# An expert layer with 128 token slots per expert instead of 96

## The reference

```
def moe_swiglu(h, router_w, router_b, w1, w3, w2):      # h: 256 tokens x 1024
    logits = h @ router_w + router_b
    top_val, top_idx = lax.top_k(logits, 2)             # 2 of 8 experts for each token
    top_p = softmax(top_val)
    combine = sum(one_hot(top_idx, 8) * top_p[..., None], axis=-2)
    for e in range(8):                                  # w1, w3: 1024 x 3584, w2: 3584 x 1024
        out = out + combine[..., e:e+1] * ((silu(h @ w1[e]) * (h @ w3[e])) @ w2[e])
```

## Time and profile before

| what | value |
|---|---|
| time, median of three runs | 2379.73 us |
| their range | 2379.34 to 2382.87 us |
| the profiled execution's own time | 2381.21 us |
| its span, first to last instruction | 2379.4 us |
| mean granted TensorE clock, share of full | 0.979 |
| PE busy | 2286.7 us (96%) |
| POOL busy | 1287.2 us (54%) |
| DVE busy | 1159.3 us (49%) |
| ACT busy | 1053.5 us (44%) |
| expert stage, first rounding to last subtraction | 1329 to 2351 us of the span |

### The profile page before, as it was taken

The page is one execution under the profiler, slowest core; times in us unless marked ns, Lnnn a source line. Parts: engine busy times, 40 slices in busy tenths (PEclk is TensorE's granted clock), DMA queues, the critical chain, the costliest instruction groups (busy, mean ns, idle before and its releaser), DMA issues.

```text
span 2379.4 us, 27429 instructions
## 1 busy us (share of the span) xinstructions
PE 2286.7 (96%) x10670; PEld 1646.3 (69%) x10671; DVE 1159.3 (49%) x1372; ACT 1053.5 (44%) x1148; POOL 1287.2 (54%) x464
## 2 busy tenths in 40 slices
PE   6999999999999999899999899999999999999996
PEld 3875457664677878777797667677777777676774
DVE  3133421123101010335522687787878787878775
ACT  3222232202321222243431477666666666766664
POOL 2300013301443445440240599989898998898994
PEclk8999999999999999989999799999999999999998
DMA  7313442122233322231144699999999999999992
GB/s 279 109 54 124 148 173 89 71 89 106 89 136 141 109 93 80 80 124 36 56 193 158 266 364 344 348 341 350 340 345 344 352 357 336 352 342 347 347 346 101
DMA packets 69642, 503.17 MB, mean 211 GB/s; under 512 B 7744, under 2 KB 7872, under 8 KB 9088
## 3 DMA queue, kind: packets, MB, share of 16 engines
q1 hardware_dynamic: 68976, 497.91, 56.1%
q0 software_dynamic: 528, 3.41, 0.4%
HBM read 500.24 MB, written 1.05 MB: 211 GB/s over the span
## 4 chain that ended last, share of the span: by engine, by line
PE 50%; POOL 34%; issue 11%; ACT 2%; DVE 1%; DMA 1%; POOLq 0%; ACTq 0%; DVEq 0%; SPq 0%
POOL moe_lo L443 33%; PE bank L702 14%; PE bank L687 10%; PE bank L689 9%; PE bank L688 9%; PE pv_bank L702 2%; PE bank L853 2%; PE turned L872 1%; ACT H_NEW L1250 1%; DMA slab<-in_w_mod 1%; PE bank L857 1%; DMA moe_slab<-in_moe_up 0%; DVE SQ_SUM L1627 0%; PE bank L800 0%; POOL w_lo L413 0%
## 5 line engine op out<-in xcount | busy, mean ns | idle before, releaser
L443 POOL TENSOR_TENSOR moe_lo<-moe_slab,moe_hi 128x512 fp32r<-128x512 f32 x336 | 921.8, 2769 | 180.4 <-ACT moe_hi L1437 179.0
L443 DVE TENSOR_TENSOR moe_lo<-moe_slab,moe_hi 128x1536 fp32r<-128x1536 f32 x336 | 692.3, 2065 | 177.6 <-ACT moe_hi L1437 175.1
L413 POOL TENSOR_TENSOR w_lo<-slab,w_hi 128x2048 fp32r<-128x2048 f32 (+2 forms) x72 | 304.1, 4225 | 802.4 <-ACT w_hi L1214 802.3
L1437 ACT ACTIVATE moe_hi<-moe_slab 128x2048 fp32r<-128x2048 f32 x336 | 629.2, 1906 | 0.0
L687 PE MATMUL bank<-moe_hi,HE_HI 128*96 128x512 f32 x896 | 361.1, 403 | 9.0 <-issue 5.3
L689 PE MATMUL bank<-moe_hi,HE_LO 128*96 128x512 f32 x896 | 353.9, 395 | 0.0
L688 PE MATMUL bank<-moe_lo,HE_HI 128*96 128x512 f32 x896 | 352.7, 394 | 0.0
L687 PE MATMUL bank<-H_HI,w_hi 128*128 128x512 f32 (+1 forms) x880 | 326.5, 371 | 15.5 <-POOL H_LO L599 14.9
L688 PE MATMUL bank<-H_LO,w_hi 128*128 128x512 f32 (+1 forms) x880 | 319.8, 363 | 0.0
L689 PE MATMUL bank<-H_HI,w_lo 128*128 128x512 f32 (+1 forms) x880 | 319.6, 363 | 0.0
L1214 ACT ACTIVATE w_hi<-slab 128x2048 fp32r<-128x2048 f32 (+1 forms) x72 | 135.5, 1884 | 173.6 <-PE bank L689 114.0
(11 more groups left out here) (190 smaller groups left out, 2530.8 us busy)
## 6 DMA issues: line engine op xcount, KB each, us to landing
moe_slab<-in_moe_up SPq DMA_DIRECT2D x224, 1024.0 KB, 4.8
moe_slab<-in_moe_w SPq DMA_DIRECT2D x112, 1024.0 KB, 4.9
slab<-in_w_mod SPq DMA_DIRECT2D x48, 1024.0 KB, 4.8
slab<-in_w_in SPq DMA_DIRECT2D x38, 1024.0 KB, 4.8
slab<-in_ffn_w SPq DMA_DIRECT2D x30, 1024.0 KB, 4.8
slab<-in_w_proj SPq DMA_DIRECT2D x8, 1024.0 KB, 6.9
slab<-in_w_out SPq DMA_DIRECT2D x8, 1024.0 KB, 4.8
slab<-in_ffn_w SPq DMA_DIRECT2D x4, 768.0 KB, 4.2
```

Source lines behind the costliest of these rows:

```text
L413: engine.tensor_tensor(lo, raw, hi.bitcast(F32), ALU.subtract).then_inc(done, 1)
L443: engine.tensor_tensor(moe_lo[n][:, blocks, :], moe_slab[k % MOE_RING][:, blocks, :], moe_hi[n][:, blocks, :].bitcast(F32), ALU.subtract). ...
L1437: af(moe_hi[k % MOE_SPLIT][:], moe_slab[k % MOE_RING][:], ACT.Copy).then_inc(moe_hi_ready, 1)
```

## The change

An expert's tokens get 128 slots. The number of passes falls from three (0 to 95, 96 to 191, 192 to 255) to two (0 to 127, 128 to 255). The tiles above grow by a third in `SLOTS`; three of them get new places, and the constant row of slot numbers, `iota`, has 256 columns instead of 288. The order of work on every engine stays as it was.

```
-SLOTS = 96
+SLOTS = 128
 PASSES = -(-S // SLOTS)
...
         HE_HI = at("HE_HI", 132, [P, 2, DC, SLOTS], F32R)
-        HE_LO = at("HE_LO", 138, [P, 2, DC, SLOTS], F32R)
+        HE_LO = at("HE_LO", 140, [P, 2, DC, SLOTS], F32R)
         SE = at("SE", 166, [SLOTS, 2, 256])
         GT = at("GT", 168, [SLOTS, 2, 256])
-        GE_HI = at("GE_HI", 170, [P, 2, 2, SLOTS], F32R)
-        GE_LO = at("GE_LO", 171.5, [P, 2, 2, SLOTS], F32R)
+        GE_HI = at("GE_HI", 160, [P, 2, 2, SLOTS], F32R)
+        GE_LO = at("GE_LO", 162, [P, 2, 2, SLOTS], F32R)
         YTOK = at("YTOK", 173, [SLOTS, D])
         ONEHOT = at("ONEHOT", 177, [P, 2, SLOTS])
         WEIGHTED = at("WEIGHTED", 178, [P, 2, SLOTS])
```

## The result

| | before | after |
|---|---|---|
| median of 17 runs each | 2380.08 us | 2384.84 us |
| range | 2378.11 to 2384.14 | 2382.41 to 2388.65 |
| ratio, with its 95% interval | | 1.0018 (1.001 to 1.0025) |
| span of the profiled execution | 2379.4 us | 2386.3 us |

The changed kernel is slower by about 0.18%, 4.8 us by the medians (2.4 to 6.0 by the interval). The forecast was 4.9 us less. The time lies in the range given, but the forecast had the wrong sign.

The account below looks back on a forecast made before the run. TensorE was taken to bound scatter, weights and gather steps; TensorE, a copy loop and GpSimd plain ones. Six full experts -4.0, first -0.3, last -0.7, start +0.1: -4.9 off 2379.7, given as 2375 us, range 2367 to 2388.

Parts of the forecast that it names:

- HE copies: Longer HE_HI and HE_LO copies push ScalarE's later roundings at g = 13: +0.10 us per full expert, bounds 0 and 0.2.
- Matmul spacing: Expert-stage matmuls go from 0.2314 to 0.2267 us apart with 128 stationary columns: 36 x 4.7 ns = 0.17 us less per step.
- The longer weight load: Loading 128 stationary columns takes 192 ns, not 163; shorter than a matmul spacing, so taken as hidden.
- rival C: The weight load's extra 29 ns shows in each of 4,032 spacings: +117 us, 2497 us; chance 0.01.
- Transposes: Transposes of gated rows stream 128 identity columns instead of 96: +0.05 us per step, bounds 0.03 and 0.06.
- Plain steps: Steps without added work go from 8.50 to 8.48 us, GpSimd's own bound: -0.02 us each, bounds -0.12 and +0.02.
- The loop: In plain steps, transposes through GE_HI, rounding copy and GpSimd's subtraction to a later slab's first matmul: +0.10 us, slack 0.06.
- g = 1, 8, 9: Steps with the YTOK copy (g = 1) and the wait for GE_LO (g = 8 and 9): +0.04 and +0.02 us.
- SE, GT, YTOK and SCATTER grow in partitions, not in columns: 0: Copies into these four tiles were to cost nothing more, having more partitions but the same columns.
- Gather, passes, DMA: Gather's matmuls and the dropped, never-run passes change nothing: 0 us each; DMA share 0.91 now, 375 GB/s at share 1.
- A: Rival: the matmul spacing stays at 0.2314 us, so longer transposes and copies only cost: +7.4 us, 2387 us; chance 0.20.
- D: Rival: gathers cost 0.8 us per expert and the HE copies 0.2, eating the gain: +1.4 us, 2381 us; chance 0.13.

Follow-up runs that it names:

- e3: Changed kernel with the gather, the transposes of gated rows and the HE and GE copies back at 96 columns, the matmuls' stationary tiles staying at 128: 2379.04 us.
- e11: Changed kernel with the two matmuls of each scatter quarter issued right behind the transposes instead of twelve matmuls later: 2385.29 us, one run.
- e2: Changed kernel with only the gated rows' transposes and the copies GE_HI and GE_LO back at 96 columns: 2378.70 us.
- e7: Changed kernel with the HE copies (ScalarE, VectorE) and ScalarE's YTOK and SCATTER copies issued ahead of the transposed gate's copies: 2375.74 us.
- e4: Gathers and HE copies of 128 columns, expert matmuls, transposes and GE copies of 96 as before the change, tiles placed as after it: 2379.24 us.
- e5: e3 with the silu tile SE and the gated tile GT made for 96 partitions only: 2375.96 us.
- e1: Changed kernel with only the gather and the copies HE_HI and HE_LO back at 96 columns: 2383.56 us.
- e12: Changed kernel with 112 slots instead of 128: 2384.61 us, one run.

## Why the prediction was wrong

It said -0.66 us for a full expert, and it was +0.64. The 1.30 between them lie, step by step, in g = 0 (0.37, with the forecast's 0.10 for the HE copies counted there), the four scatter steps (0.31), g = 6, 10 and 11 (0.20), g = 8 and 9 (0.16), g = 1 (0.11), g = 12 (0.07), g = 7 (0.05) and g = 13 (0.02).

*Matmul spacing: the step that failed.* "The other 35 spacings fill 8.10: 0.2314 each" was taken to 0.2267 for all 36, the first behind the transposes (0.29) too. The mechanism was right, the stationary tile and not the traffic makes the difference (e3 against before), and 0.2267 is reached. But the dense rows are taken far behind an interruption. In a scatter step after the change some 20 of 36 spacings are at 227; 5 behind the transposes and 9 behind the scatter are at 231 to 232 on average, as with 96. That is 14 x 4.7 ns = 0.07 of the 0.08 us by which a scatter step missed its forecast (-0.04, not -0.12). e11 bears it out by taking one interruption away.

*The longer weight load.* "Both are shorter than a spacing, and the dense layer hides 192 under 227" holds in the run of equal matmuls, and rival C did not come. Behind the transposes it is not hidden: 290 became 314 ns, where the load grew by 26 (163 to 189). Per step that is 0.025 us. Behind the scatter nothing of it shows: the first spacing there went from 424 to 418 ns.

*Transposes.* +0.05 was forecast, and transposes with the first matmul did go from 0.40 to 0.45 us. But only 0.023 of it is the transpose (85 to 108 ns); the rest is the exposed load. The sum was right by luck, by two errors that cancel.

*Plain steps.* The loop was sized rightly: copies +0.05 and +0.07, slack gone, TensorE held for 0.02 by GpSimd's subtraction (a spacing of 0.245, the matmul 0.146 us behind GpSimd's end). What was missed is that the short wait is itself an interruption: it costs 0.08 in the first spacing behind it, and the ten matmuls after it run at 231. In place of 8.48 stands 8.55. With the gated rows' copies at 96 columns the wait is gone, and the step is 8.43 (e2, e3), which is below the 8.48 that "a plain step can't stay below".

*g = 1, 8, 9.* +0.04 and +0.02 were forecast, +0.15 and +0.18 (0.11 and 0.07) measured. The copies' growth is as worked out; most of the give-back by shrunk spacings was not there, by the same error, and at g = 1 some 0.05 beyond that stays open. e7 shows that at g = 1 and 8 it is the single ScalarE copy between GE_HI and the next rounding that sets the length. At g = 8 the forecast left that out: it had the loop, lengthened by a single copy, at g = 1 alone.

*HE copies.* +0.10 (0 to 0.2) was forecast, in g = 13. The cost lies in g = 0: 0.24 in e4 alone, and 0.12 to 0.28 per expert beside the 128-wide tiles. The trace had the length of the copies; what stood behind them was not followed into the next step.

*Who goes first.* Nothing in the prediction answers to the other 0.2 us of g = 0. "SE, GT, YTOK and SCATTER grow in partitions, not in columns: 0" is true of their own times and false of what follows them (e3 to e5: 0.22 us per expert, and 2.6 us in the medians against before).

*Gather, passes, DMA.* The gather cost nothing, as the earlier trace rows had it: e2 and e3 differ in its columns, and both have 11.98 at g = 12. With a share of 0.93 where it was 0.91, and 341 GB/s as before, DMA did not come into it:

```profile
1345.00:2350.00 1005.00, 995.12 (x4535) 805.85 (x4534) 828.72 (x657) 692.87 (x580) 864.57 (x332) 1.00 0.93 341
```

Of the rivals, A came nearest in time (2387) but not by its mechanism: it had the spacing at 0.231 throughout, and scatter steps of 9.41. The truth lies between A and the forecast, matmul by matmul. All of the forecast hung on a gain of 4.7 ns in 231 being had everywhere, and neither A nor D asked what becomes of it where it is had in part.

## What to carry to other kernels

A spacing read from a long run of equal matmuls holds for long runs only: count the matmuls between two interruptions before multiplying, and price each kind of interruption (a transpose, other matmuls, a wait of 20 ns) by its own first spacing and what follows it. Where two engines' work on the same slab starts within a tenth of a microsecond, a change in the instruction ahead can turn round who is slowed; look at the difference of the starts, and give the engine that the chain needs a clear lead. A single copy that stands between a step's own copy and the work that waits behind it is worth moving into time in which the engine idles: moving three of them gave 0.58 us per expert at 96 slots and 1.19 at 128, as much as the slots cost or more.

## What the runs showed of the hardware

**VectorE and GpSimd in turn.** Over the 14 profiled kernels, wherever VectorE's subtraction (1536 elements per partition, two inputs) starts 0.04 to 0.2 us ahead of GpSimd's on the same slab (2538 pairs), VectorE takes 1.75 to 1.85 us and GpSimd 2.79 to 2.89. Where GpSimd starts 0.13 to 0.55 us ahead (117 pairs), GpSimd takes 1.27 to 1.48 and VectorE 2.50 to 2.77. Between these it hangs on the instruction that VectorE is just leaving: with GpSimd 0.05 ahead, VectorE kept 1.75 us behind a GT of 96 partitions (e5, before) and fell to 2.86 behind one of 128 (e1, e3); with 112 partitions and 0.08 it kept its pace (e12), and with 96 even at 0.12 (e4). Why is not shown. The Trainium skill (GPSIMD Engine Reference, section "1. Specifications") says that GpSimd shares its SBUF interfaces with VectorE and contends with instructions of two SBUF inputs; the traces agree, and put the price in these pairs at some 1.5 us for GpSimd's 512 columns or 0.8 to 1.1 for VectorE's 1536, paid by one of the two. Further apart both can be slow: in the 904 pairs in which VectorE starts 1 to 2 us ahead, the medians are 2.73 and 2.81 us, since each meets another of the other engine's subtractions.

**Spacing by columns of the stationary tile.** 231 ns with 96 and 112, 227 with 128, and this only from the seventh spacing behind the transposes or the eleventh behind the scatter on. What settles there is not shown. e4, whose stationary tiles have 96 columns in rows of 128, has plain steps of 8.46, 0.04 under before, 1 ns per matmul. Tiles of 96 columns in the new layout are thus a little quicker; whether by the longer rows or by the new places is not shown. So of the 4.7 ns about 1 may belong to the layout and not to the 128 columns.

**A drop of the clock at the start of the stage.** In the profiled execution after the change the first step takes 12.61 us instead of 11.08. The table by stretches shows the clock falling there; its columns are the stretch, its length, busy times of PE, PEld, DVE, ACT and POOL, the granted clock, and the share and rate of DMA:

```profile
1344.00:1348.00 4.00, 1.66 (x9) 1.19 (x8) 3.49 (x2) 4.00 (x4) 3.48 (x2) 1.00 0.20 82
1348.00:1352.00 4.00, 4.00 (x12) 3.10 (x11) 3.72 (x3) 0.30 (x1) 4.00 (x2) 0.57 0.92 297
```

TensorE was busy for only 1.66 of 4 us (it waits 2.3 us for GpSimd's subtraction), and in the next four the granted clock is 0.57 on average, a mixture of 1.2 and 2.4 GHz. The same wait is in the trace of before without a drop, and the drop is in e7 and e11 too, but in none of the other profiled kernels, six of which have 128-wide matmuls as well. Whether it belongs to 128 slots or to the execution is open; it is no part of the 4.8 us worked out above.
